# A two-layer encoder on one core: first weight unit split by halves, conditioning slices half a slot later, attention head loop reordered with two output banks

## What is computed

```
mod = silu(c) @ ada_w + ada_b;  sh1, sc1, g1, sh2, sc2, g2 = split(mod, 6)
layer 0: x += g1 * retention(modulate(rmsnorm(x), sh1, sc1))     # w_in 1024 x 6144, w_out 2048 x 1024
         x += g2 * (silu(h @ w_gate) * (h @ w_up)) @ w_down      # dense, inner width 2816
layer 1: x += g1 * attention(...)    # 8 query heads, 2 key/value heads of 128; q and k normalised
         x += g2 * moe_top2_of_8(...)                            # inner width 3584 for each expert
out = modulate(rmsnorm(x), fsh, fsc)
```

## Time and profile before

| | us |
|---|---|
| median of 3 runs | 1586.56 (1585.43 to 1588.83) |
| the profiled execution | 1589.74 |
| its span in the trace | 1587.9 |

### The profile page before, as it was taken

One profiled execution on the slowest core, in us unless ns is written; L12 is line 12 of the kernel. 1 busy time (PEld: TensorE's weight loads), 2 busy tenths in 40 slices (PEclk: granted clock), 3 DMA queues, 4 the chain that ended last, 5 costly groups with the idle time before them and its releaser, 6 DMA issues.

```text
span 1587.9 us, 20528 instructions
## 1 busy us (share of the span) xinstructions
PE 1531.4 (96%) x6818; PEld 1228.9 (77%) x6818; DVE 1335.5 (84%) x1071; ACT 982.5 (62%) x811; POOL 198.1 (12%) x188
## 2 busy tenths in 40 slices
PE   6999998899999799999999999999999999999997
PEld 6777676677777588778888888888888888888885
DVE  6799878877778779998888988988988888888898
ACT  4554434343446555677777767777776777777674
POOL 0499700000020011001001001000000000000320
PEclk9999999999999999999999999999999999999999
DMA  9989735788874179999999999999999999999993
GB/s 342 380 287 350 274 105 201 272 300 298 295 249 166 46 260 344 391 346 369 375 361 367 379 358 363 386 352 365 385 353 367 381 369 352 381 369 352 390 394 141
DMA packets 238896, 508.70 MB, mean 320 GB/s; under 512 B 15494, under 2 KB 38150, under 8 KB 238728
## 3 DMA queue, kind: packets, MB, share of 16 engines
q1 hardware_dynamic: 233824, 491.52, 85.6%
q0 software_dynamic: 4448, 14.55, 2.5%
q10 hardware_dynamic: 584, 2.11, 0.3%
HBM read 502.12 MB, written 7.87 MB: 321 GB/s over the span
## 4 chain that ended last, share of the span: by engine, by line
PE 82%; DVE 10%; ACT 3%; DMA 3%; issue 2%; SPq 0%; DVEq 0%; ACTq 0%
PE bank L1969 25%; PE bank L1970 25%; PE bank L1971 25%; PE bank L2388 2%; DVE lo L1212 1%; DVE lo L1719 1%; DVE hs L1292 1%; DMA stage<-in_l_moe_w_gate 1%; PE bank L1947 1%; PE bank L2075 1%; DVE ada_acc L1224 1%; DVE lo L1609 1%; PE bank L2257 1%; ACT hi L739 0%; DMA stage<-in_l_moe_w_up 0%
## 5 line engine op out<-in xcount | busy, mean ns | idle before, releaser
L1719 DVE TENSOR_TENSOR lo<-stage,hi 128x2048 fp32r<-128x2048 f32 x168 | 388.2, 2319 | 39.6 <-ACT hi L1070 38.8
L1070 ACT CAST hi<-stage 128x2048 fp32r<-128x2048 f32 x168 | 321.3, 1914 | 107.7 <-DMA stage<-in_l_moe_w_up 86.5
L1970 PE MATMUL bank<-lo,hg_hi 128*128 128x512 f32 x896 | 353.7, 395 | 0.0
L739 ACT CAST hi<-stage 128x2048 fp32r<-128x2048 f32 x69 | 131.6, 1910 | 130.8 <-PE bank L1971 103.7
L1970 PEld LDWEIGHTS bank<-lo,hg_hi 128*128 128x128 f32 x896 | 168.9, 189 | 36.8
L1212 DVE TENSOR_TENSOR lo<-stage,hi 128x2048 fp32r<-128x2048 f32 x69 | 159.2, 2311 | 30.5 <-ACT hi L739 24.7
L1719 DVE TENSOR_TENSOR lo<-stage,hi_h 128x2048 fp32r<-128x2048 f32 x56 | 128.3, 2292 | 66.2 <-ACT hi_h L1070 66.2
L1969 PE MATMUL bank<-hi,hg_hi 128*128 128x512 f32 x452 | 178.9, 396 | 0.3 <-issue 0.2
L1971 PE MATMUL bank<-hi,hg_lo 128*128 128x512 f32 x452 | 179.0, 396 | 0.0
L1970 PE MATMUL bank<-lo,eaT_hi 128*128 128x512 f32 x448 | 177.4, 396 | 0.0
L1969 PE MATMUL bank<-hi,hT_hi 128*128 128x512 f32 x400 | 165.8, 415 | 8.5 <-DVE hT_lo L1267 3.4
(11 more groups left out here) (354 smaller groups left out, 2789.1 us busy)
## 6 DMA issues: line engine op xcount, KB each, us to landing
stage<-in_l_moe_w_gate SPq DMA_DIRECT2D x224, 512.0 KB, 5.0
stage<-in_l_moe_w_up SPq DMA_DIRECT2D x224, 512.0 KB, 5.2
stage<-in_l_moe_w_down SPq DMA_DIRECT2D x224, 512.0 KB, 4.9
ada_w<-in_l_ada_w SPq DMA_DIRECT2D x40, 1024.0 KB, 5.5
stage<-in_l_ret_w_in SPq DMA_DIRECT2D x48, 512.0 KB, 6.9
stage<-in_l_ffn_w_gate SPq DMA_DIRECT2D x22, 512.0 KB, 7.9
stage<-in_l_ffn_w_up SPq DMA_DIRECT2D x22, 512.0 KB, 8.7
stage<-in_l_ffn_w_down SPq DMA_DIRECT2D x22, 512.0 KB, 6.5
```

What stands on the lines that cost most here:

```text
L739: nc.scalar.copy(hi_of(b), stage[:, b % RING, :]).then_inc(hi_done, 1)
L1070: nc.scalar.copy(hi_e(b), stage[:, b % RING, :]).then_inc(hi_done, 1)
L1719: nc.vector.tensor_tensor(lo[:, b % RING, :], stage[:, b % RING, :], hi_e(b).bitcast(F32), ALU.subtract).then_inc(lo_done, 1)
L1970: mm(dst_ap, a_hi, w_lo, start=False, stop=False)
```

## The change

It has three parts and computes the same.

1. *Start.* The first unit's second transfer has its own semaphore; ACT casts and DVE subtracts it in two halves, DVE ahead of `columns_pre(0)`. `low(U_RET + 3)` moves ahead of `columns_pre(1)`.
2. *Dense layer.* `fin(6)` moves behind the first `low` of the layer. The second half of each slice moves one slot later on SP and DVE, `ada_sum` and `ada_take` with it.
3. *Attention.* The last slice's eight steps (L1563) leave the head loop and go among DVE's work on k and q. In the loop ACT does `soft(h+2)` before `aq_take` and `o_take`; `qkv_squares(2)` goes ahead of the loop with its square-root table; values alternate between banks 7 and 3 (the last one 4), so `a_values(h)` waits for `o_low(h-2)`; `low_o(2)`, `low_o(3)` and `high_o(3)` move to the loop's end.

```diff
+O_BANK = (7, 3, 7, 3, 7, 3, 7, 4)
-            load_in(0)
+            first = stage[:, 0, :].rearrange("p (k n) -> p k n", k=4)
+            sp.dma_start(first[:, 0:2, :], w_in_v[:, 0:2, 0:CB]).then_inc(w_first, 16)
+            sp.sem_inc(w_load[0], 16)
+            sp.dma_start(first[:, 2:4, :], w_in_v[:, 2:4, 0:CB]).then_inc(w_load[0], 16)
...
+            load_dense(0, 0)
+            load_ada(A_FF, 0, l1_ada_w, l1_ada_b, 0)
+            load_dense(0, 1)
+            load_ada(A_FF, 1, l1_ada_w, l1_ada_b, 0)
+            load_ada(A_FF + 1, 0, l1_ada_w, l1_ada_b, AC)
+            with sp.Fori(0, (N_FF - 1) // 2 - 1) as it:
+                for q in range(2, 4):
+                    load_dense(it, q)
+                    load_ada(A_FF + q - 1, 1, l1_ada_w, l1_ada_b, it * (2 * AC) + (q - 1) * AC, it * 2)
+                    load_ada(A_FF + q, 0, l1_ada_w, l1_ada_b, it * (2 * AC) + q * AC, it * 2)
...
@@ ACT @@
-            high(U_RET)
+            act.wait_ge(w_first, 16)
+            nc.scalar.copy(hi[:, 0, 0:UW // 2], stage[:, 0, 0:UW // 2]).then_inc(hi_half, 1)
+            act.wait_ge(w_load[0], 32)
+            nc.scalar.copy(hi[:, 0, UW // 2:UW], stage[:, 0, UW // 2:UW]).then_inc(hi_done, 1)
...
             soft(1)
-            act.wait_ge(w_used, RING + U_QKV + 5)
-            high_o(3)
+            ada_take(A_AT - 1, mod_at((A_AT - 1 - A_L1) * AC))
+            nc.scalar.activation(warm[:, 5:6], eps, ACT.Sqrt)
+            act.wait_ge(w_used, RING + U_QKV + 6)
+            qkv_squares(2)
             qkv_copy(2)
             for h in range(AH):
                 pT_take(h)
+                if h == 0:
+                    head_roots(2)
+                if h + 2 < AH:
+                    soft(h + 2)
                 if h in (1, 3):
                     aq_take(3 + h // 2)
                 if h:
                     o_take(h - 1)
...
@@ DVE, dense @@
+            f_units(0, 0, between=lambda: fin(6))
+            fin(7)
+            ada(A_FF, 0)
+            f_units(0, 1)
+            ada_slot(0, 1)          # ada(A_FF + q - 1, 1), then ada(A_FF + q, 0)
...
@@ PE, attention @@
             def a_values(h):
                 pe.wait_ge(at_pT, h + 1)
-                if h:
-                    pe.wait_ge(o_lo, h)
+                if h >= 2:
+                    pe.wait_ge(o_lo, h - 1)
...
             aq_turn(2)
+            ada_sum(A_AT - 1)
             qkv_half(5, 0)
```

More of the change, by code:

```diff
@@ L1342, in _ @@
             pre(1, range(2, 8))
+            low(U_RET + 3)
             columns_pre(1)
@@ L1503, in f_units @@
                 low(b, it * 6)
+                if between is not None:
+                    between()
                 f_mul(cc - 1)
@@ L1507, in f_units, with ada_slot @@
                 low(b + 2, it * 6)
-            def f_pair(it):
+            def ada_slot(it, q):
+                ada(A_FF + q - 1, 1, it * 2)
+                ada(A_FF + q, 0, it * 2)
+            f_units(0, 0, between=lambda: fin(6))
[3 more added lines that the diff above has]
+            ada_slot(0, 1)
+            last = (N_FF - 1) // 2 - 1
+            with dve.Fori(1, last) as it:
                 for q in range(2):
                     f_units(it, q)
[L1512 to L1524, removed]
+                    ada_slot(it, q)
             f_units(last, 0)
-            for half in range(2):
-                ada(A_AT - 2, half)
+            ada_slot(last, 0)
+            scale(2, A_L1 + 4)
             f_units(last, 1)
-            scale(2, A_L1 + 4)
+            ada(A_AT - 2, 1)
             low(U_QKV - 1)
@@ L1610, in low_o @@
                                         ALU.subtract).then_inc(lo_done, 1)
+            low(U_QKV + 2)
+            for k in range(2):
+                ada_step(A_AT - 1, k)
+            low(U_QKV + 3)
+            for k in range(2, 5):
+                ada_step(A_AT - 1, k)
             link(head_rope(AH, AKV, ktab, TT))
@@ L1619, in _ @@
             low(U_QKV + 5)
+            for k in range(5, KT):
+                ada_step(A_AT - 1, k)
             head_rope(0, 2, qtab, 2 * TT).then_inc(arope, 1)
@@ L1654, in _ @@
             row_max(3)
-            ada_step(A_AT - 1, 0)
-            o_low(0)
+            head_rope(4, 2, qtab, 3 * TT).then_inc(arope, 1)
             head_scales(2)
             row_norm(2)
+            o_low(0)
             row_max(4)
-            ada_step(A_AT - 1, 1)
-            ada_step(A_AT - 1, 2)
+            row_norm(3)
+            head_rope(6, 2, qtab, 3 * TT).then_inc(arope, 1)
             o_low(1)
[L1663 to L1679, removed]
+            for h in range(2, 5):
+                row_max(h + 3)
+                row_norm(h + 2)
+                o_low(h)
+            scale(3, A_AT)
+            low_o(2)
+            row_norm(7)
             o_low(5)
@@ L1682, in _ @@
             nc.vector.tensor_tensor(wr_hl[:, :, E:2 * E], wr[:, :, :], wr_hl[:, :, 0:E].bitcast(F32), ALU.subtract).then_inc(r_w, 1)
-            row_norm(7)
-            scale(3, A_AT)
+            low_o(3)
             o_low(6)
@@ L2301, in _ @@
                 a_turn(h)
+                if h == 1:
+                    pe.wait_ge(a_out, 1 + A_AT)
                 if h in (1, 3):
```

67 lines of the change are left out of this document (30 added, 37 removed).

## The result

The changed kernel takes 1576.03 us (median of 4 runs, 1575.49 to 1579.41) against 1587.13 (4 runs beside them): ratio 0.9933, 95% interval 0.9919 to 0.9948. That is 11.1 us less, where 14.4 were forecast and 1565.5 to 1580.5 was the range. The profiled execution took 1576.01 us, its span is 1574.2.

A forecast was written before the change was run, and what follows sets the result against it. TensorE was taken to bound the kernel, with waits at the start, dense entry and head loop that also lower its clock. Terms 4.5 + 6.3 + 3.6 = 14.4 us gave a median of 1572.2, range 1565.5 to 1580.5.

The forecast's parts named there:

- (A): Rival: the attention gives nothing, later rotations of q and k spending its 9.4 us; time about 1576; chance 0.14.
- (B): Rival: the start's lead is absorbed because units 4 and 5 are not ready sooner; 1576.7; chance 0.08.
- Start, first half: At the start: the first unit's low part in halves brings the first product to 26.4, about 2.0 us sooner.
- Start, second half: At the start: unit 3's early low part lets its product start at about 48.4; 4.5 us, bounds 1 and 6.
- I expect a cold stretch again: At the start: the wait from about 42 to 48.4 brings low clock, so 4.5 of 6.1 us is counted.
- Dense entry: At the dense layer's entry: earlier transfers let gate/up start 4.6 us sooner; with clock 6.3, bounds 4 and 7.
- I take 2.1: At the dense entry: gain from cold clock no longer lost, 2.1 of the 2.4 us at 300 to 310.
- Attention: Loop starts 3.0 us later and is 9.4 shorter, less 2.8 for clock: 3.6, bounds 0.5 and 6.4.
- I give 2.8 of it back: In the attention: 2.8 of the 6.4 us gain given back for new cold stretches, leaving 3.6.
- (C): Rival: no change, as the first experts' units wait for transfers and the lead is lost; 1586.6; chance 0.04.
- (D): Rival: slower, TensorE waiting 2.9 us in each of eight dense slots; 1595.4; chance 0.05.
- (E): Rival: the attention's table switch costs its drain, making that term 2.3 us smaller; 1574.5; chance 0.02.

The follow-up runs named there:

- start_only: The kernel before with only the start of the change (first unit in halves, unit 3's low part early): 1586.33 us, ratio 0.9992.
- Before_again: The kernel before once more, nothing edited, to see which low-clock stretches return; its dense entry took 41.3 us.
- no_attention: The changed kernel with the attention as before, start and dense layer as changed: 1580.95 us, ratio 0.9962 to the kernel before.

## Why the forecast held, and where its sizes were off

The direction is right and all three places gave something, but the measured time, 1576.03, is nearer to what rivals A (1576) and B (1576.7) say than to the forecast's 1572.2. The range was wide enough to hold all three, so the time alone does not bear the forecast out; the stages do, with the sizes below.

*Start, first half.* Forecast: first product at 26.4. It came at 27.75 to 27.99 in four traces, the changed kernel's first among them, and at 26.2 to 26.5 in the other eight. The step did not count the eight filling matmuls behind the first sums, which end at 28.2 where low clock falls on them. As said there, this lead is not kept.

*Start, second half.* `pm` at 46.5 (46.47), unit 3 at 48.4 (48.65) and its use (55.6 forecast; the cast at 55.04 waits for the transfer instead) are right. The sentence "I expect a cold stretch again" is right in some executions and wrong in others: 4.5 forecast, 5.1 in the first trace, 3.9 on average, 1.5 at worst. It is a spread, which I carried as one number. And the runs of start_only, at 1.3 with 3.5 as the upper end, make even 3.9 doubtful: by them this term of 4.5 is the one furthest off.

*Dense entry.* The mechanism is right: the early issue, the wait of 0.31, 1.00 of clock at 300. By the traces this term is the furthest off, 6.3 against 4.5 on average, and two of its parts failed. The wait's 4.6 was 3.8: from the `low` of unit 36 to the end of `f_turn` the old kernel takes 19.7 to 19.9 us and the new one, with no low clock there, 15.9 to 16.0, since TensorE still waits 0.31 and the transpose takes 0.66 for the 0.44 of the forecast. The other is "I take 2.1": the clock's share came from one execution, in which the earlier trace rows show 0.66. Before_again has 0.83 in the same ten us (3.4 us of low clock instead of 6.8) and its entry is 1.3 shorter. In six of ten new traces the entry takes 38.0 or 38.2 instead of 36.7; in them low clock fell between 276 and 286, part of it ahead of the cut at unit 36, and `f_turn` ends 1.4 us later than in the other four. So the gain lies between 3.1 (41.3 - 38.2) and 6.0 (42.7 - 36.7). The gate transfer went out 14.7 us sooner, 9.5 beyond the start's lead, for the "some 9" of the text.

*Attention.* Ahead of the loop: 2.37 for the forecast 2.2, and the sum. Waits in the loop: 6.01 for 6.6, the largest 2.51 for 2.65 and at `aq_turn(3)`, as said. The step "I give 2.8 of it back" for low clock in the loop was wrong: none fell there in any trace of this loop unedited. One of 3.4 fell at the layer's entry (467 to 470.5) in two of these five. From the third head's scores to `ao_unit(1, 1)` the loop took 34.98 to 35.01 us for the walked 34.4, and the old one 43.1 on average for the 43.8 of one execution: 8.2 gained for 9.4. Ahead of it the cost was 3.7 for 3.0. So 4.5 instead of 3.6 is partly luck: the walk was 1.9 too high, and the 2.8 taken back for low clock that did not come more than made up for it.

Why the loop has become shorter is only half settled. In single traces the bank is worth 0.7, the steps nothing net (their nine runs leave that open) and ACT's new order costs; each was undone alone, so parts that hide each other are not excluded. The trace of the kernel before points at the rest. Its two longest waits in the loop are for VectorE's `row_norm`:

```profile
524.36 1.28 ACT L971 ACT_TABLE_LOAD   x1
527.30 1.11 PE L2247 MATMUL bank<-cst,prob 128*128 128x128 f32 x4 [2.05 <-DVE prob L1638]
533.83 1.02 PE L2247 MATMUL bank<-cst,prob 128*128 128x128 f32 x4 [2.56 <-DVE prob L1638]
```

Ahead of the first, VectorE itself waits 1.06 us for ACT's square roots, which come behind that table load; ahead of the second, it does the rotation of the last two heads (530.97 to 533.05) before `row_norm(3)`. In the changed kernel the square roots' table is loaded at 509.26, ahead of the loop, that last rotation stands behind `row_norm(3)`, and no transpose of a head waits for `row_norm` in its trace. What VectorE's new order and the squares ahead of the loop are worth by themselves was not tried.

*The router* was in no term. Its length rises with the low clock in it, and in both traces of the changed kernel that was 10.2 us, in the two of before 3.4 and 6.8. But three kernels with the new start and dense entry and a new attention had 3.4, and start_only with the old one 10.2. I call it chance that costs 0.6 on average, not a part of the change; nine traces against five do not settle it.

*The rivals.* (A) had the attention give nothing: 4.5, and the 3.0 to 4.9 between no_attention and the changed kernel, speak against it. Its condition, a cold stretch behind every wait over 2 us, does not hold either: the waits of 2.35 to 2.58 us ahead of the loop and of 2.51 in it brought none in five traces. (B), the start absorbed, comes true in some executions, by the clock and not by VectorE's later units (in the changed kernel TensorE has no wait over 0.3 us from 48.65 to 62), and the 1.3 us of start_only's runs are near its number. (C) is out, since the experts keep what comes to them (967.6 to 970.2 us in all traces). (D) is out by 140.9 us in every trace for the dense slots. The 2.3 of (E) has no working on record, and (E) is out: in the changed kernel the exponential behind `head_roots(2)` starts at 515.55, 0.01 after the table's load of 1.28 at 514.26; no drain there either, on the path where the Trainium skill ("ScalarE: Activation LUTs", "What ACT_TABLE_LOAD costs") would put 1.38:

```profile
514.26 1.28 ACT L1005 ACT_TABLE_LOAD   x1
515.55 0.56 ACT L1005 ACTIVATE prob<-bank,asm,ahs 128x256 f32<-128x256 f32 x1
```

## What to carry to other kernels

Walk the waits by hand from the rows: single starts and waits came out within 0.3 us where the engines' work sets them, whole stages within 0.6 to 1.2. Cost the clock apart, as a spread over executions, because the same wait brings 3.4 or 10.2 us of it or none, and compare stages cut at the same work instead of spans. An edit that bundles several reorderings may hold one that costs: here the exponentials first seem to cost 1 to 2 us of what the rest had won (97.8 against 99.0 and 100.0), in one trace that the runs neither confirm nor refute.

## What the hardware showed that I had not expected

Up to the last unit of the experts the stretches at 0.50 (1.2 instead of 2.4 GHz) are 3.4, 6.8 or 10.2 us long and lie at different places in executions of one kernel. TensorE loses about 1.55 us for each 3.4 where it has work (22.7, 24.3 and 25.8 us of router). The longest of these, 10.2 us, begin either inside a wait of over 3 us that is followed by sixteen one-column products (42.9 in start_only, whose wait ends at 43.89) or in the router's narrow products, in which TensorE is busy by its records all the time: 10.00 of 10 us from 566 to 576.
